# Layer norm of a convolution branch between attention heads: Pool adds channel tiles and squares before TensorE sums them, and the chains stand elsewhere

## The reference, cut to what matters

```python
def layernorm(x, g, b):
    xf = x.astype(jnp.float32)
    mu = jnp.mean(xf, axis=-1, keepdims=True)
    var = jnp.mean(jnp.square(xf - mu), axis=-1, keepdims=True)
    y = (xf - mu) * lax.rsqrt(var + LN_EPS)
    return (y * g.astype(jnp.float32) + b.astype(jnp.float32)).astype(x.dtype)

def conv_branch(u, hist, w_dw, b_dw, ln_g, ln_b):
    full = jnp.concatenate([hist, u], axis=1)
    c = lax.conv_general_dilated(full, w_dw[:, None, :], (1,), 'VALID', ...) + b_dw
    c = layernorm(c, ln_g, ln_b)
    c = c * jax.nn.sigmoid(c)
```

## Time and profile before

| | us |
|---|---|
| median of 3 runs | 1586.57 |
| lowest, highest | 1582.46, 1588.49 |
| profiled execution, its own time | 1586.11 |
| its span | 1584.3 |
| granted TensorE clock, mean of the span | 0.987 |

### The profile page before, as it was taken

One profiled execution on the slowest core, in us unless ns is written; L12 is line 12 of the kernel. 1 busy time (PEld: TensorE's weight loads), 2 busy tenths in 40 slices (PEclk: granted clock), 3 DMA queues, 4 the chain that ended last, 5 costly groups with the idle time before them and its releaser, 6 DMA issues.

```text
span 1584.3 us, 22226 instructions
## 1 busy us (share of the span) xinstructions
PE 1514.5 (96%) x8544; PEld 1268.1 (80%) x8544; DVE 676.7 (43%) x1322; ACT 603.6 (38%) x1081; POOL 425.7 (27%) x445
## 2 busy tenths in 40 slices
PE   7998999999899998889999999999999999999995
PEld 4466356654888774578799999999999999999995
DVE  2438367888935444445542222222222222222234
ACT  4217458885457645644431121212213021121211
POOL 3232014432623113323322212211211212112124
PEclk9999999999999989999999999999999999999998
DMA  6021132355580005440011111111111111111112
GB/s 239 1 58 58 54 83 88 150 132 83 199 257 35 2 1 226 160 166 1 1 54 41 45 49 40 45 48 40 49 43 40 50 42 40 48 45 40 52 42 100
DMA packets 95636, 116.66 MB, mean 74 GB/s; under 512 B 15142, under 2 KB 80758, under 8 KB 92996
## 3 DMA queue, kind: packets, MB, share of 16 engines
q1 hardware_dynamic: 92076, 94.72, 19.8%
q0 software_dynamic: 3488, 20.98, 3.6%
HBM read 95.05 MB, written 20.95 MB: 73 GB/s over the span
## 4 chain that ended last, share of the span: by engine, by line
PE 54%; POOL 1%; DVE 1%; DMA 0%; issue 0%; ACT 0%; DVEq 0%; POOLq 0%; ACTq 0%
PE ps L2357 18%; PE ps L2359 18%; PE ps L2358 18%; PE ps L2392 0%; POOL y L2252 0%; DVE y L2527 0%; DMA out_y_p<-y 0%; POOL wlo L2216 0%; PE ps L2444 0%; DVE y L2537 0%; POOL stat L2227 0%; ACT whi L2266 0%; ACT hhi L2324 0%; POOL stat L2223 0%; DVEq L2526 0%
## 5 line engine op out<-in xcount | busy, mean ns | idle before, releaser
L2216 POOL TENSOR_TENSOR wlo<-wraw,whi 128x1024 fp32r<-128x1024 f32 x62 | 148.9, 2402 | 566.5 <-ACT whi L2266 566.4
L2358 PE MATMUL ps<-xlo,whi 128*128 128x384 f32 (+1 forms) x768 | 250.3, 326 | 0.0
L2357 PE MATMUL ps<-hhi,whi 128*128 128x384 f32 (+1 forms) x720 | 235.1, 327 | 0.8 <-POOL wlo L2216 0.8
L2359 PE MATMUL ps<-hhi,wlo 128*128 128x384 f32 (+1 forms) x720 | 235.2, 327 | 0.0
L2358 PE MATMUL ps<-hlo,whi 128*128 128x384 f32 (+1 forms) x720 | 234.9, 326 | 0.0
L2266 ACT CAST whi<-wraw 128x1024 fp32r<-128x1024 f32 x62 | 65.2, 1052 | 293.8 <-PE ps L2359 293.8
L2504 DVE TENSOR_TENSOR rel<-rel 128x384 f32<-128x384 f32 (+1 forms) x96 | 51.5, 537 | 283.6 <-ACT rel L2332 283.6
L2332 ACT ACTIVATE rel<-ps 128x384 f32<-128x384 f32 (+1 forms) x96 | 45.3, 473 | 264.3 <-PE ps L2359 264.3
L2358 PEld LDWEIGHTS ps<-xlo,whi 128*128 128x128 f32 x768 | 144.1, 188 | 0.0
L2357 PEld LDWEIGHTS ps<-hhi,whi 128*128 128x128 f32 x720 | 135.1, 188 | 1.1 <-POOL wlo L2216 1.1
L2359 PEld LDWEIGHTS ps<-hhi,wlo 128*128 128x128 f32 x720 | 135.1, 188 | 0.0
(11 more groups left out here) (313 smaller groups left out, 2810.2 us busy)
## 6 DMA issues: line engine op xcount, KB each, us to landing
wraw<-in_w_up SPq DMA_DIRECT2D x32, 512.0 KB, 4.0
wraw<-in_w_down SPq DMA_DIRECT2D x32, 512.0 KB, 3.4
taps<-qT SPq DMA_DIRECT2D x9, 960.0 KB, 4.0
hT<-taps SPq DMA_DIRECT2D x7, 960.0 KB, 4.9
x<-in_x SPq DMA_DIRECT2D x13, 512.0 KB, 7.4
w<-in_w_u SPq DMA_DIRECT2D x2, 2048.0 KB, 8.4
wo_raw<-in_w_out SPq DMA_DIRECT2D x8, 512.0 KB, 3.5
out_y_p<-y SPq DMA_DIRECT2D x8, 512.0 KB, 2.6
```

Source lines behind the costliest of these rows:

```text
L2216: nc.gpsimd.tensor_tensor(wlo_of(j, last), raw[:], whi_of(j, last), ALU.subtract).then_inc(s_wlo, 1)
L2357: nc.tensor.matmul(o, wh, xh, start=first, stop=False)
L2358: nc.tensor.matmul(o, wh, xl, start=False, stop=False)
L2359: return nc.tensor.matmul(o, wl, xh, start=False, stop=last)
```

## The change

Two kinds of work move from TensorE to Pool, and the stages stand at other steps.

- `add_channels`: Pool adds the four channel tiles of `conv` into `csum` (the first 1088 columns of `probS`) in three instructions, once for all chunks, in round r = 4 behind `split_query(4)`. `channel_sums(n)` is then a single product of ones and `csum`, and waits for these additions in place of the bias.
- `add_squares(n)`: Pool adds the squares of channel tiles 2 and 3 to those of 0 and 1, in place, in round r = 5 + n between `split_query(r)` and `inverse_sigma(n)`. `row_squares(n)` then has two products for each row tile instead of four, and waits for this addition in place of the squares.
- The chunks start at steps 33, 39 and 46 instead of 33, 40 and 47. `row_squares` stands at stage 7 (was 5), `variance` at 8 (was 6), `on_diagonal` at 10 (was 7), `spread_sigma` at 11 (was 8), `normalise` at 12 (was 9). `channel_sums`, `centre` and `squares` keep stages 0, 1 and 3.

```diff
--- before.py
+++ after.py
@@ -1323,9 +1323,10 @@
     rwide = sb_in(st, "rwide", [P, GRP * P])
     spread = sb_in(st, "spread", [P, 3, P])
     knew = sb_in(st, "knew", [P, NB * NT])
-
-    LNJ = 4 * NH + 1
+    csum = probS[:, 0:T]
+
     LNB = NBLK // 2
+    LN_AT = [LNB * NH + 1, LNB * NH + 7, LNB * NH + 14]
     sq = mask[:, MK_OFF[LNB]:MK_OFF[LNB] + 2 * CC * 384].bitcast(F32).rearrange("p (c t) -> p c t", c=CC)
     vpage = [vpage0, m["vpage1"], vpage0, kpage]
 
@@ -1368,6 +1369,7 @@
     s_sum = sem("a_sum")
     s_cen = sem("a_cen")
     s_sq = sem("a_sq")
+    s_add = sem("a_add")
     s_var = sem("a_var")
     s_ve = sem("a_ve")
     s_rs = sem("a_rs")
@@ -1417,7 +1419,7 @@
 
     ln_tiles = [[i for i in range(RT) if t0 <= i * P < t0 + w] for t0, w in TCH]
 
-    ln_step = lambda j, after: (j - LNJ - after) // 7 if (j - LNJ - after) % 7 == 0 and 0 <= (j - LNJ - after) // 7 < len(TCH) else None
+    ln_step = lambda j, after: LN_AT.index(j - after) if j - after in LN_AT else None
 
     with nc.Block() as block:
         @block.sync
@@ -1510,6 +1512,19 @@
                 nc.gpsimd.tensor_tensor(lnv[:, 1, cols], lnv[:, 0, cols], neghalf[:].broadcast_to([P, len(tiles)]),
                                         ALU.pow).then_inc(s_rs, 1)
 
+            def add_channels():
+
+                pool.wait_ge(s_cb, CC)
+                nc.gpsimd.tensor_tensor(csum, conv[:, 0, :], conv[:, 1, :], ALU.add).then_inc(s_add, 1)
+                for c in range(2, CC):
+                    pool.wait_ge(s_add, c - 1)
+                    nc.gpsimd.tensor_tensor(csum, csum, conv[:, c, :], ALU.add).then_inc(s_add, 1)
+
+            def add_squares(n):
+                w = TCH[n][1]
+                pool.wait_ge(s_sq, n + 1)
+                nc.gpsimd.tensor_tensor(sq[:, 0:2, 0:w], sq[:, 0:2, 0:w], sq[:, 2:4, 0:w], ALU.add).then_inc(s_add, 1)
+
             for r in range(2, NBLK):
                 if r >= 6:
                     pool.wait_ge(s_rs, r - 5)
@@ -1518,8 +1533,14 @@
                     pool.wait_ge(s_ql, NKV * (r + 1))
                     split_out(r - 2, s_wo[0], 32)
                     pool.wait_ge(s_ol, r - 1)
+                if r == 4:
+                    pool.wait_ge(s_ql, NKV * (r + 1))
+                    add_channels()
+                    pool.wait_ge(s_add, CC - 1)
                 if r >= 5:
                     pool.wait_ge(s_ql, NKV * (r + 1))
+                    add_squares(r - 5)
+                    pool.wait_ge(s_add, CC + r - 5)
                     inverse_sigma(r - 5)
 
             def load_keys(pr):
@@ -1715,23 +1736,20 @@
             def channel_sums(n):
                 t0, w = TCH[n]
                 pe.wait_ge(s_c, 16)
-                pe.wait_ge(s_cb, CC)
+                pe.wait_ge(s_add, CC - 1)
                 pe.wait_ge(s_m, LNB * NH - 1 + n % 2)
                 if n >= 2:
                     pe.wait_ge(s_nm, n - 1)
-                for c in range(CC):
-                    last = nc.tensor.matmul(ln_wide[n][:, 0:w], ones[:], conv[:, c, t0:t0 + w],
-                                            start=(c == 0), stop=(c == CC - 1))
-                last.then_inc(s_sum, 1)
+                nc.tensor.matmul(ln_wide[n][:, 0:w], ones[:], csum[:, t0:t0 + w], start=True, stop=True).then_inc(s_sum, 1)
 
             def row_squares(n):
 
-                pe.wait_ge(s_sq, n + 1)
+                pe.wait_ge(s_add, CC + n)
                 for q, i in enumerate(ln_tiles[n]):
                     r = rows_of(i)
-                    for c in range(CC):
+                    for c in range(2):
                         last = nc.tensor.matmul(ln_var[n][0:r, i:i + 1], sq[:, c, q * P:q * P + r], ones[:, 0:1],
-                                                start=(c == 0), stop=(c == CC - 1))
+                                                start=(c == 0), stop=(c == 1))
                 last.then_inc(s_var, 1)
 
             def spread_sigma(n):
@@ -1750,10 +1768,10 @@
                     turn(j - LAG)
                 if ln_step(j, 0) is not None:
                     channel_sums(ln_step(j, 0))
-                if ln_step(j, 5) is not None:
-                    row_squares(ln_step(j, 5))
-                if ln_step(j, 8) is not None:
-                    spread_sigma(ln_step(j, 8))
+                if ln_step(j, 7) is not None:
+                    row_squares(ln_step(j, 7))
+                if ln_step(j, 11) is not None:
+                    spread_sigma(ln_step(j, 11))
                 if j in value_steps:
                     values(*value_steps[j])
                 if j >= WIDE and (j - WIDE) % NH == 0:
@@ -1929,7 +1947,7 @@
                         dve.wait_ge(s_co, 16 * (c // 2 + 1))
                         nc.vector.tensor_scalar(conv[:, c, :], conv[:, c, :], gvec[:, 2 * KC + c:2 * KC + c + 1], None,
                                                 ALU.add).then_inc(s_cb, 1)
-                    for after, work in ((1, centre), (6, variance), (7, on_diagonal), (9, normalise)):
+                    for after, work in ((1, centre), (8, variance), (10, on_diagonal), (12, normalise)):
                         if ln_step(j, after) is not None:
                             work(ln_step(j, after))
                 if j >= NH and j % NH == 1:
```

## The result

| | before | after |
|---|---|---|
| median | 1587.53 (4 runs) | 1569.00 (4 runs) |
| lowest, highest | 1582.46, 1588.50 | 1568.59, 1572.77 |
| profiled execution | 1586.11 | 1569.07 |
| its span, mean granted clock | 1584.3, 0.987 | 1566.9, 0.992 |

What follows compares the result with a forecast made beforehand. TensorE's own sequence was taken as the bound (busy 1514.5 of 1584.3 us). Terms: -5.9 - 5.7 - 2.4 - 5.0 + 2.5 + 1.5 = -15.0 us, giving 1571.5 us on the median's footing, 0.95% faster, range 1565 to 1578.5.

Steps and rivals of the forecast that it cites:

- Rival 3: Behind the heads, TensorE's waits for copies and pages give part of the gain back: 1580 to 1584 us; chance 0.06.
- A: TensorE's channel sums: one product in place of four leaves a quarter of 7.8 us, -5.9 us.
- B: TensorE's single-column products: half as many, 10.0 us down to 4.3 at full clock, -5.7 us.
- C: TensorE's waits for ScalarE's squares ahead of the single-column products go, as these stand two heads later: -2.4 us.
- D: Three half-clock stretches of TensorE among the heads (3.2, 6.5, 6.4 us) go if the clock never falls: -5.0 us.
- G: One short clock fall remains among the heads, most likely in chunk 1 behind a 0.65 us wait: +1.5 us.
- E: Pool's three channel additions, 7.6 us together, end near 523, before the first channel sum at 533.6: cost 0.
- F: New TensorE waits from the moved chains, at four tight places (1.0, 0.65, 0.7, 0.2 us): +2.5 us, bounds 0 and 6.
- Rival 1: The clock falls three times as before behind the single-column products, despite fewer of them: 1575.5 us; chance 0.26.
- Rival 2: Pool's chunk-1 squares addition locks out VectorE's third chunk-0 diagonal; spread waits 2.8 us, another long clock fall: 1576 us; chance 0.10.
- Idle alone: TensorE's clock falls only from array idle between bursts, so removing the waits for squares would hold it: -16.5 us.
- Rival 4: New waits keep the clock at 0.50 from the first product (head 40) to the last spread (head 57): 1588.5 us; chance 0.03.

Runs made afterwards that it cites:

- e1: Kernel before with only Pool's channel additions, so one channel product a chunk; squares, single-column products and steps as before: 1584.65 us, ratio 0.9967.
- e4: Changed kernel without Pool's addition of the squares: four squares products, 24 single-column records a chunk, at the new steps: 1582.77 us, ratio 0.9971 to before.
- e2: Kernel before with only the new steps; four channel products and four squares products, nothing added by Pool: 1584.44 us, ratio 0.9986.
- e3: Changed kernel with its chains put back to the old steps, Pool's additions kept: 1589.70 us, ratio 1.0004 to before.
- e8: Changed kernel with Pool's three channel additions made twice, the result the same: 1568.52 us, ratio 0.9872 to before.
- e9: Changed kernel with Pool's query split of round 6 ahead of the power of chunk 0 instead of behind it: 1566.04 us, ratio 0.9863 to before.
- e6: Changed kernel with diagonals, spread and normalise one step later and the third chunk at step 47 instead of 46: 1575.40 us, ratio 0.9910 to before.

## Why the prediction was right, point by point

- **Bound.** TensorE's own sequence was the bound, and the gain moved to the end whole: 16.0 us at head 63, 17.4 at the end of the span. Rival 3 (given back later) did not occur; what was left behind the heads was a gain of 1.2 us, from the clock.
- **A**, -5.9: measured -5.5 in the timeline, 5.1 in e1. Right.
- **B**, -5.7: -5.9 between starts in the profiles; 3.8 of work in e4 against the 4.1 in it that are not clock. Right.
- **C**, -2.4: as summed in the profile. In e2, where 1.9 us of the new waits stand against it, the part without the clock fell by 1.7 us, somewhat more than the difference of 0.5. What I did not see is that it was the condition for the rest: e3, without it, gained nothing.
- **D and G**, -5.0 and +1.5: -4.3 within the heads against the -3.5 of both. One short fall of 3.1 us, at chunk 1, behind the 0.65 us wait that I had named (0.62 measured). In the profiled pair that is right, but the place of the fall is partly luck: e8 has the same wait and records and no fall there. The step that was too simple is to take three stretches of 3.2, 6.5 and 6.4 us as the price of the kernel before. That execution was one of the better ones: about 41 us of half clock in all, where the median of 57 was 51 and the highest 64. Against the median the change keeps 24 us of half clock, worth 24 x 0.365 = 9 us, while the part without the clock fell by 11.2. That makes 20 us by this estimate, where the medians differ by 19.6 (1588.60, all 57) or 18.5 (1587.53, the four beside the changed kernel), instead of the 15 of the sum; the two profiled executions differ by 17.0.
- **E**, 0: confirmed by e8 with twice the additions. The two estimates of Pool's speed (2.5 and 1.8 us) were 2.57 and 1.82.
- **F**, +2.5: 0.92, 0.62, 0.56 and 0 against 1.0, 0.65, 0.7 and 0.2, together 2.1. The mechanism of the first was tested by e9. One slip in the range: the sum without G and with half of F is -17.8, not -19, which is the sum without G and F; the range as given goes lower than this working carries.
- **Rival 1** (three falls as before): not in the changed kernel. With 24 records at the new steps it is what happened (e2, e4).
- **Rival 2** (the lock at one more place): the occasion did not arise. The third diagonal ended at 556.07 and Pool's addition began at 556.66, because it still had 0.69 us to wait for ScalarE's squares. That Pool's split holds up VectorE is shown: with the split elsewhere the diagonals went from 2.53 to 0.67 us. The Trainium skill (SBUF — State Buffer, "SBUF: two separate sides"), which the prediction named for the lock, agrees with that.
- **Idle alone**, by the Trainium skill (TensorE: Matmul & The Clock Gate, "HAM oscillation"): the measurements differ from it where chunk 0's run of 24 single-column records with no wait ahead still brought the clock down (e2, e4). They agree with it in that idle adds to it: e3, with 62 us of half clock against 27 at the same number of records (its steps differ, too), and, less strictly, e6.
- **Rival 4** (the low level stays over 23 us): did not happen to the changed kernel, and I gave it 0.03. But the mechanism exists and was underrated: 30.4, 27.1 and 26.9 us in one piece in e1, e4 and e6, the last being a variant with less waiting by design. The price per microsecond of half clock was near, 0.41 in D against 0.365 from the line: e6 has 17 us more of it than the changed kernel in the median and is 6.4 us slower.

What stays open: why a run of the same length and wait brings a fall in one execution and none in another (changed kernel and e8), why the low level lasts 3 us in one case and 27 to 30 in another, and what brings or lengthens the falls behind the heads, at 642 to 683 us.

## What to carry to other kernels

Where TensorE is busy all the time, look at its granted clock by stretches before counting instructions: a run of tiny products behind a wait can cost more in the work that follows than in itself, and that price varies from run to run. Give sums over tiles to an idle engine, but only together with moving the consumer far enough back that TensorE does not wait for them; parts of the change alone gained 0 to 0.3% here, all together 1.05%. Then look for what the helper's other work blocks: putting Pool's query split ahead of the power freed VectorE's diagonals and gave about 3 us more by the medians, 1.2 of them apart from the clock.

## What the runs showed of the hardware

The granted clock stayed at 0.50 for 30.4, 27.1 and 26.9 us (e1, e4, e6) while TensorE was over 95% busy with small products, so work alone does not bring it back at once. It fell behind a run of 24 single-column records (2.74 us) with no wait ahead (e2, e4). With 12 records behind a wait of 0.62 or 0.63 us it fell in one execution (after) and not in another (e8). And executions of the kernel before spread over 13 us (1582 to 1595) almost only by this: 0.35 us of span for each microsecond of half clock, and a standard deviation of 1.0 us (4.6 from lowest to highest) left when that is taken off. Three additions of 1088 float32 columns on Pool (2.57 us for the first) cost nothing where Pool was idle, and neither did six (1568.5 against 1569.0 us, e8).
